# Moving the weight splits of the attention stages: other steps on ScalarE and VectorE, two of them to GpSimd

## The reference

```python
for i in range(DEPTH):                       # first block, 2 layers
    h = rms_norm(x, norm_mix_pre[i])
    z = h @ w_in[i]
    c_q, c_kv, k_rope, q_c, k_c, v_c, g_a, g_b, g_c = jnp.split(z, split_points, axis=-1)
    o_a = mla_attention(c_q, c_kv, k_rope, ...)          # 8 heads
    o_b = fourier_mix(h)
    o_c = windowed_gqa(q_c, k_c, v_c, positions, sink)   # 8 heads, ALiBi distances, a sink
    merged = (jax.nn.sigmoid(g_a) * (o_a @ w_branch_a[i])
              + jax.nn.sigmoid(g_b) * (o_b @ w_branch_b[i])
              + jax.nn.sigmoid(g_c) * (o_c @ w_branch_c[i]))
    ...                                      # projection, feed forward, embedding
# second block: feed forward, attention, feed forward, in each of 2 layers;
# both attentions have 16 heads of 64 with a causal mask
```

## Time and profile before

| | |
|---|---|
| median of 3 runs | 1939.96 us (1939.25 to 1940.83) |
| the profiled execution | 1939.25 us, of which the span of the profile is 1937.6 us |
| PE busy | 1888.8 us, 97% of the span |
| PE weight loads busy | 1540.1 us, 79% |
| DVE busy | 1108.2 us, 57% |
| ACT busy | 958.3 us, 49% |
| POOL busy | 149.1 us, 8% |
| granted TensorE clock | 0.997 of full speed |

### The profile page before, as it was taken

One profiled execution on the slowest core, in us unless ns is written; L12 is line 12 of the kernel. 1 busy time (PEld: TensorE's weight loads), 2 busy tenths in 40 slices (PEclk: granted clock), 3 DMA queues, 4 the chain that ended last, 5 costly groups with the idle time before them and its releaser, 6 DMA issues.

```text
span 1937.6 us, 26218 instructions
## 1 busy us (share of the span) xinstructions
PE 1888.8 (97%) x9054; PEld 1540.1 (79%) x9054; DVE 1108.2 (57%) x1344; ACT 958.3 (49%) x1256; POOL 149.1 (8%) x258
## 2 busy tenths in 40 slices
PE   8999999999998999999999999999999999999998
PEld 7767888887786788888788887688888888868886
DVE  6555664557666566445755555745564555665554
ACT  5655454445565445444544445644454444565443
POOL 4200010000301001000200012000011000100000
PEclk9999999999999999999999999999999999999999
DMA  6324555554413555555665554365555554525552
GB/s 221 111 98 159 194 196 195 195 188 161 163 66 131 179 174 203 188 195 179 196 206 179 189 185 152 109 211 195 180 187 198 195 180 166 196 98 186 183 180 102
DMA packets 204844, 332.73 MB, mean 172 GB/s; under 512 B 11344, under 2 KB 150224, under 8 KB 204752
## 3 DMA queue, kind: packets, MB, share of 16 engines
q1 hardware_dynamic: 200240, 319.33, 48.8%
q0 software_dynamic: 3120, 11.02, 1.7%
q10 hardware_dynamic: 1392, 1.21, 0.2%
HBM read 330.47 MB, written 1.05 MB: 171 GB/s over the span
## 4 chain that ended last, share of the span: by engine, by line
PE 84%; issue 6%; DVE 4%; ACT 4%; POOL 1%; DMA 1%; SPq 0%; DVEq 0%; ACTq 0%; POOLq 0%
PE ps L554 26%; PE ps L542 26%; PE ps L549 26%; PE ps L576 3%; ACT whi L1207 2%; ACT prob L1304 1%; PE ps L720 1%; DVE wlo L1663 1%; PE ps L732 1%; PE ps L748 1%; DVE soft L1790 1%; DMA raw<-w_in_dram 1%; DVE prob L1802 0%; DVE prob L1783 0%; DVE prob L1775 0%
## 5 line engine op out<-in xcount | busy, mean ns | idle before, releaser
L1663 DVE TENSOR_TENSOR wlo<-raw,whi 128x2048 fp32r<-128x2048 f32 (+2 forms) x308 | 695.3, 2257 | 538.0 <-ACT whi L1207 537.5
L1207 ACT ACTIVATE whi<-raw 128x2048 fp32r<-128x2048 f32 (+2 forms) x308 | 581.0, 1886 | 427.7 <-PE ps L554 425.7
L542 PE MATMUL ps<-whi,act_hi 128*128 128x512 f32 (+1 forms) x1632 | 444.5, 393 | 4.7 <-issue 2.2
L549 PE MATMUL ps<-wlo,act_hi 128*128 128x512 f32 (+1 forms) x1632 | 442.4, 390 | 0.1
L554 PE MATMUL ps<-whi,act_lo 128*128 128x512 f32 (+1 forms) x1632 | 435.7, 388 | 0.7 <-DVE act_lo L1669 0.7
L554 PEld LDWEIGHTS ps<-whi,act_lo 128*128 128x128 f32 x1632 | 304.9, 188 | 64.9 <-DVE act_lo L1669 1.5
L549 PEld LDWEIGHTS ps<-wlo,act_hi 128*128 128x128 f32 x1632 | 303.1, 188 | 63.6 <-issue 1.1
L542 PEld LDWEIGHTS ps<-whi,act_hi 128*128 128x128 f32 x1632 | 298.2, 188 | 62.9 <-issue 2.4
L1251 ACT ACTIVATE hid<-ps,stat 128x256 f32<-128x256 f32 x132 | 62.7, 475 | 282.8 <-PE ps L576 197.3
L2218 POOL TENSOR_TENSOR stat<-stat,eps 128x1 f32<-128x1 f32 x44 | 22.9, 520 | 1479.3 <-ACT prob L1238 1479.0
L1715 DVE SCALAR_TENSOR_TENSOR hid<-ps,stat,hid 128x256 f32<-128x256 f32 x132 | 63.5, 481 | 123.0 <-ACT hid L1251 123.0
(11 more groups left out here) (202 smaller groups left out, 1622.0 us busy)
## 6 DMA issues: line engine op xcount, KB each, us to landing
raw<-ffn_w_gate_dram SPq DMA_DIRECT2D x88, 512.0 KB, 4.0
raw<-ffn_w_up_dram SPq DMA_DIRECT2D x88, 512.0 KB, 5.0
raw<-ffn_w_down_dram SPq DMA_DIRECT2D x88, 512.0 KB, 3.9
raw<-w_in_dram SPq DMA_DIRECT2D x64, 512.0 KB, 4.4
raw<-w_ffn_gate_dram SPq DMA_DIRECT2D x44, 512.0 KB, 3.9
raw<-w_ffn_up_dram SPq DMA_DIRECT2D x44, 512.0 KB, 4.9
raw<-w_ffn_down_dram SPq DMA_DIRECT2D x44, 512.0 KB, 3.9
raw<-a_w_qkv_dram SPq DMA_DIRECT2D x24, 512.0 KB, 4.4
```

Of the source, the lines that this page charges most:

```text
L542: nc.tensor.matmul(o, hi, a, start=start and i == 0, stop=False)
L549: nc.tensor.matmul(o, hi, a, start=False, stop=False)
L1207: nc.scalar.activation(whi[:, u % SLOTS, 0:words], raw[:, u % SLOTS, 0:words], ACT.Copy)\
L1663: nc.vector.tensor_tensor(wlo[:, u % SLOTS, 0:words], raw[:, u % SLOTS, 0:words], whi[:, u % SLOTS, 0:words].bitcast(F32), ALU.subtract)\
```

## The change

The change has four parts.

1. In the first block ACT takes `exps(s + 1)` ahead of `probs_turned(s)` for odd s too, as it did for even s. Where ACT has gates to take (L1400), it now splits its weight unit first and takes the gates behind it.
2. The rest of units 10 and 11 (`wlo`), which DVE wrote in `shifts` of heads 3 and 5, is now written by POOL, right behind the first two distance products. DVE only waits for both at `x == 0`, behind head 7.
3. In the two attentions of the second block the splits stand in other steps: on ACT one before the loop and in steps 2, 4, 8 and 12 before, now in steps 2, 6, 8, 10 and 14; on DVE in steps 1, 5, 7, 11 and 16 before, now in steps 3, 7, 9, 11 and 15.
4. There DVE's steps with an even s also have another order: `normalise(s - 1)` stood ahead of `shifts(s)` and `pair_lo`, and now stands behind both.

```diff
                     x -= 2 * FGROUPS - 1
+                    if x != 7:
+                        split(1)
                     if x in (1, 3):
                         for t in range(T):
                             half_there(HF_GB + x - 1 + t)
                             ...
-                    if x != 7:
-                        split(1)
...
                 for s in range(heads + 1):
-                    if s % 2:
-                        probs_turned(s, TN_HEAD + s, False)
                     head_exps(s + 1)
                     ...
                     if s < heads:
-                        if s % 2 == 0:
-                            probs_turned(s, TN_HEAD + s, False)
+                        probs_turned(s, TN_HEAD + s, False)
...
-                split(1)
                 for s in range(1, H2 + 2):
...
-                    if s in (2, 4, 8, 12):
+                    if s in (2, 6, 8, 10, 14):
                         split(1)
...
-                    if i in (3, 5):
-                        split(1)
                     if i < heads:
                         normalise(i, ("score_read_a", i + 1) if i < H1 else ("expd", i - H1 + 1), i >= H1)
...
+                    if x == 0:
+
+                        done[0] += 2
+                        dve.wait_ge(sem("lo"), w.at("lo", done[0]))
                     if x != 7:
                         split(1)
...
                 for s in range(H2 + 3):
-                    if 1 <= s <= H2 and s % 2 == 0:
-                        normalise(sc + s - 1, ("expd", sc + s), causal=True)
                     if s < H2:
                         shifts(sc + s, add=mask, scale=float(HD2) ** -0.5, causal=True)
                     if s >= 4 and s % 2 == 0:
 
                         pair = (s - 3) // 2
                         pair_lo(sc // 2 + pair, o2_lo[:, pair, :], o2_hi[:, pair, :])
-                    if s <= H2 and s % 2:
+                    if 1 <= s <= H2:
                         normalise(sc + s - 1, ("expd", sc + s), causal=True)
-                    if s in (1, 5, 7, 11, 16):
+                    if s in (3, 7, 9, 11, 15):
                         split(1)
...
+                    if i == 1:
+
+                        for u in (U_GATE_B, U_GATE_B + 1):
+                            pool.wait_ge(sem("lo"), w.at("lo", u))
+                            pool.wait_ge(sem("hi"), w.at("hi", u + 1))
+                            nc.gpsimd.tensor_tensor(wlo[:, u % SLOTS, :], raw[:, u % SLOTS, :],
+                                                    whi[:, u % SLOTS, :].bitcast(F32), ALU.subtract)\
+                                .then_inc(sem("lo"), 1)
```

## The result

The changed kernel is slower: median 1960.66 us (4 runs, 1958.01 to 1964.16) against 1940.39 us (4 runs), ratio 1.0102, 95% interval 1.0090 to 1.0114, or +20.3 us. The forecast was 1953, with a range of 1943 to 1960. The sign was right; the size was missed by 7.7 us, and the time lies just outside the range. (All 21 executions on record lie between 1957.1 and 1964.2, with a median of 1959.8, so the edge of the range is within their spread.)

A forecast was written before the change was run, and what follows sets the result against it. PE was taken as the bound, busy 1888.8 of 1937.6 us, with rings through DVE and ACT making it wait. From 1939.25, -8.3, +8.2 and +13.2 gave 1952.4, so a median of 1953, range 1943 to 1960.

The forecast's parts named there:

- The sign: Whole kernel: slower by over 0.2%, chance 0.86.
- Part 2, 2.05 us for each POOL operation: Early heads of a layer: POOL's 4.5 us subtraction holds up DVE's scaling, so PE loses 2.05 us four times, 8.2.
- Parts 3 and 4: Second block's attentions: a closed loop through PE, ACT and DVE loses 6.6 us per attention, 13.2 for both.
- a ring of 6.94 us: Second block: one turn from transposition through copy, splits, maximum, pair's rest and scaling takes 6.94 us against PE's own 5.24.
- the sum: Whole kernel: 1939.25 - 8.3 + 8.2 + 13.2 = 1952.4 us; the runs' median lies 0.7 higher, 1953.
- Part 1, -4.2 us per layer: Later heads of a layer: splitting ahead of the gates shortens the ACT-DVE loop, gaining 4.2 us per layer, 8.3 for two.
- at the step of head 12: Later heads: the copy of the transposition, now behind the exponentials and ahead of the split, adds 0.5 us there.
- so these waits lie inside the same time: Later heads: PE's new waits for gates (about 0.6 us) and head 13's late copy don't delay head 15.
- the clock falls as well: New waits at head 15 and behind POOL: two to four falls, 3 to 6 us more, 1956 to 1959; chance 0.12.
- POOL cheap: Early heads: POOL takes 2.9 us or DVE's scaling slips past; total 1945 to 1947 us; chance 0.18.
- faster: Second block's loop doesn't close, staying under PE's 5.24 us, and POOL's hold is absorbed: about 1931 us; chance 0.09.
- no change: Whole kernel: gains and losses cancel within 0.2%, with the second block at a third of its figure; chance 0.05.

The follow-up runs named there:

- where the waits are filled: Only the two rests moved to POOL, plus 10 dummy transpositions ahead of heads 3 and 5, against the kernel before: 1950.08 us, ratio 1.0041, +8.7 us.
- four of 1.29 to 1.34: Only the two rests moved to POOL, each written in four pieces of 512 words, against the kernel before: 1939.99 against 1940.17 us, ratio 0.9997.
- the places of the splits alone: Only the steps of the second block's splits changed, DVE's order as before, against the kernel before: 1953.02 us, ratio 1.0068, +12.9 us.
- part 1 alone: Only ACT's order in the first block's layers changed (late copy, split ahead of gates), against the kernel before: 1932.61 us, ratio 0.9955, -8.5 us.
- the full change with its waits filled: The changed kernel with dummy transpositions in PE's longest waits, against the kernel before: 1953.20 us, ratio 1.0061, +12.1 us.
- The gates alone: Only gates moved behind ACT's split, against the kernel before: 1929.29 us, ratio 0.9941; with 12 dummy transpositions ahead of head 14: 1928.05 us, ratio 0.9933.
- +11.2 us: Only the rests of units 10 and 11 moved from DVE to POOL, against the kernel before: 1952.24 us, ratio 1.0054.
- the whole second block changed: Only the second block's splits and DVE's order changed, against the kernel before: 1955.79 against 1941.07 us, ratio 1.0074, +14.7 us.
- its order alone: Only DVE's order in the second block changed, splits as before, against the kernel before: 1942.09 us, ratio 1.0009, +1.9 us.
- it filled: Only the second block changed, plus 20 dummy transpositions ahead of each attention's last head, against the kernel before: 1954.99 us, ratio 1.0068, +13.7 us.
- its last split moved: Only the second block changed, with DVE's last split in step 16, against the kernel before: 1954.51 against 1941.33 us, +13.2 us.

## Why the prediction was right in sign and wrong in size

By its own steps, against the profiled execution:

- **Part 2, 2.05 us for each POOL operation, 8.2 in all: right.** 2.0 each where the waits are filled. The duration was 4.57 us for my 4.5, and the scaling was stopped and not slowed. The lock that the Trainium skill (SBUF — State Buffer, "SBUF: two separate sides") states is what the runs show too: 3.92 us for the scalings beside one POOL operation of 4.57, and 1.68 beside four of 1.29 to 1.34.
- **Parts 3 and 4, a ring of 6.94 us and +6.6 us per attention: right in number** (6.93, and 6.62 and 6.59). Only in part right in what it was put down to: I took DVE's maximum and the pair's rest as links, without which there would be a ring of 6.0, but the places of the splits alone give a second ring of 6.81 and 5.2 of the 6.6 us. This didn't change the sum.
- **Part 1, -4.2 us per layer: mis-sized both ways.** With part 1 alone, where the clock held, it was 4.8 us; in the full change with its waits filled 4.3 and 4.4, close to the forecast; in the full change as it is only 3.3. The gates alone give 5.9, and the late copy takes 1.1 back. I had 0.5 for it, at the step of head 12 only. The distances of the maxima show where it is: at the two steps with gates 7.29 us in the kernel with the gates alone and 7.77 with the late copy, at the step of head 12 7.65 and 7.76.
- **The step that failed** is in part 1 and in the sum: what a wait of PE costs. Of PE's new waits in the later heads I wrote that the ring, not PE, sets when head 15 is ready, "so these waits lie inside the same time", and the sum charged every other wait with its own length only. Their effect on the clock behind them was put at nothing in the sum and left to a rival. Their lengths were about right (3.18 us for 3.4 at the last head, 1.48 and 0.41 for 2 behind POOL). What they do to the work behind them wasn't in it: six stretches of half clock where PE is the bound. From the first table: 5.65 and 5.40 us in the early heads against 4.05 with the waits filled, 1.6 and 1.3; a gain of 3.3 us in the later heads against 4.3 and 4.4 with the waits filled, twice 1.1; and from head 15 of an attention to the next stage 11.3 to 12.8 and 19.4 to 20.9, twice 1.5. Together 8.1 us. Without it the change costs 20.9 - 8.1 = 12.8, close to the 13.1 of the sum, and to the 13.5 - 0.8 = 12.7 of the filled kernel.
- **The rival "the clock falls as well" was the case**, and I gave it 0.12. It was undersized as well: two to four falls, 3 to 6 us, where there were six and 8.1 us. I had the evidence and read half of it. The earlier trace rows show the clock at 0.58 from 141 to 144, behind a wait of 2.07 us at 140.20. In the kernel before, PE still waited 2.5 us for DVE at head 14 behind this fall, so it had the time to take the fall up. Part 1 takes such waits away: in the full change PE comes to head 15 without waiting for DVE, and the fall is paid.
- POOL cheap, faster, and no change are excluded by +11.2, 4.57 us and the ring.

The Trainium skill (TensorE: Matmul & The Clock Gate, "HAM oscillation — how this bites in real kernels") tells of a kernel whose PE waits some 3 to 5 us for each load and then starts its next products at the lower clock. The traces here agree at the six places, with mostly shorter waits (from 1.48 and 0.41 us to 3.18), and show waits of 3.18, 2.44 and 1.88 us without a fall at others.

What stays open is what decides, for one and the same wait, whether the clock falls. It isn't the length of the wait alone. That it can differ between executions of the same code is in the traces. The first block is the same in the kernel before and in five kernels of the experiments (the whole second block changed, its places alone, its order alone, it filled, its last split moved). In each of the six traces PE stands idle for 2.1 to 2.6 us ahead of the same products (L542, at about 480 us, between the two layers' attentions). Half clock followed in three of them and full clock in the other three. The kernel before, and the one with the order alone:

```profile
479.86 1.18 PE L542 MATMUL ps<-whi,act_hi 128*128 128x512 f32 x4 [2.19 <-issue]
...
481.04 2.07 PE L542 MATMUL ps<-whi,act_hi 128*128 128x512 f32 x4 [2.26 <-issue]
```

The same three kernels have one more fall at 163 us, behind a wait of 2.5 to 2.7 us for head 14. So one profiled execution can hold a fall or two more or fewer than the next one of the same kernel, and a difference of 2 or 3 us between two runs isn't by itself the work of an edit. The kernel before spread from 1939.3 to 1944.8 us in 21 executions on one chip, which fits this.

## What to carry to other kernels

A wait on an engine that is the bound costs its length and what the clock does behind it: look in the trace of before for such falls, also those hidden in slack, and put up to one of them (here 1.5 us) on the price of each new wait as long as those behind which they stand, as the upper end of a range, since not every such wait brings one. Dummy work in a wait that can't be removed got that part back in the full change; in the two parts and in the kernel with the gates moved the falls behind the filled waits went as well, but the times didn't resolve what that gave. When an element-wise operation moves to POOL, its length is what DVE may have to wait for; here four pieces took the whole loss away. When a split is moved so that DVE takes the unit that ACT has just split, both become links of the softmax's ring. The kernel before had two to four steps between them; how many are needed wasn't tested.

## What the runs showed of the hardware that was not expected

- DVE gets in between two POOL operations that stand back to back: scalings of 1.68 us for two instead of 3.92, for 0.56 us more on POOL (5.13 against 4.57).
- A fall of the clock isn't certain behind a wait: 3.18 us with and without, 2.44 us with and without, 1.88 us both ways in one execution. The waits of 1.2 to 1.5 us at heads 7, 9, 11 and 13 of the second block brought none; the one of 1.48 at head 3 or 5, with 0.41 more right behind it, brought one per layer.
- The fall also comes in places that the change doesn't touch: in the kernel with the gates moved, at 474.16 us, four products of L542 took 2.03 us, behind 2.29 us in which PE stood idle; the same products took 1.18 us in the kernel before, behind 2.19 us.
